# Meta tokens' products in four column quarters, attention inputs in two substeps, group sums by parity

## What is computed

```python
def first_block(...):                      # cut
    ...                                    # four mixers, x = x + rms_norm(y)
    h = rms_norm(x, pre_mlp_g[l])
    m = jnp.square(jax.nn.relu(h @ mlp_w1[l])) @ mlp_w2[l]
    x = x + rms_norm(m, post_mlp_g[l])

def second_block(...):                     # cut
    h = jnp.concatenate([meta, x], axis=1)            # 16 meta rows, then 256
    for layer in range(2):
        hn = rmsnorm(h, norm_mix[layer])
        if layer == 0:
            mix = pool_mixer(hn, pool_w[0], pool_scale[0])       # four column groups of 256
        else:
            q = rmsnorm((hn @ w_q[0]) by heads, q_norm[0])
            mix = stick_breaking(q, k_sh, v_sh) @ w_o[0]
        h = h + mix
        h = h + peer(rmsnorm(h, norm_ffn[layer]), peer_wq[layer], peer_keys[layer], ...)
        if layer == 0:
            kv = rmsnorm(h, kv_norm) @ w_kv           # keys and values for layer 1
    return h[:, N_META:]
```

## Time and profile before

| | |
|---|---|
| median of 3 timed runs | 1873.5 us (1872.88 to 1874.62) |
| profiled execution | 1869.93 us |
| its span, first to last instruction | 1867.8 us |
| mean granted TensorE clock | 0.829 of 2.4 GHz |
| busy: PE, DVE, ACT, POOL | 1380.9, 1166.1, 597.2, 548.5 us |
| HBM traffic | 678.30 MB read, 364 GB/s over the span |

### The profile page before, as it was taken

One profiled execution on the slowest core, in us unless ns is written; L12 is line 12 of the kernel. 1 busy time (PEld: TensorE's weight loads), 2 busy tenths in 40 slices (PEclk: granted clock), 3 DMA queues, 4 the chain that ended last, 5 costly groups with the idle time before them and its releaser, 6 DMA issues.

```text
span 1867.8 us, 21493 instructions
## 1 busy us (share of the span) xinstructions
PE 1380.9 (74%) x7036; PEld 559.3 (30%) x7036; DVE 1166.1 (62%) x2679; ACT 597.2 (32%) x1524; POOL 548.5 (29%) x629
## 2 busy tenths in 40 slices
PE   7979999987885556669777875596687855555666
PEld 6836666654330110123122221131232210101010
DVE  4831244037785767776688537866886478677764
ACT  2421011113443333344343333333543333332332
POOL 2001052003333333322333322332333233333332
PEclk9989999989996775689777897798897977766666
DMA  9049297617999999999999999999999999999997
GB/s 332 23 150 359 91 378 292 252 46 306 420 420 418 421 421 421 421 408 417 419 392 398 418 416 421 413 392 417 421 417 419 419 421 403 421 421 421 418 420 294
DMA packets 117982, 680.74 MB, mean 364 GB/s; under 512 B 11710, under 2 KB 13888, under 8 KB 49904
## 3 DMA queue, kind: packets, MB, share of 16 engines
q0 software_dynamic: 78336, 553.68, 71.9%
q1 hardware_dynamic: 39536, 125.71, 17.5%
HBM read 678.30 MB, written 1.05 MB: 364 GB/s over the span
## 4 chain that ended last, share of the span: by engine, by line
DMA 36%; PE 32%; DVE 12%; ACT 5%; issue 3%; DVEq 2%; POOL 2%; ACTq 1%; POOLq 0%
DMA big<-in_peer_uv,expert 32%; PE ps L585 7%; PE ps L743 6%; PE ps L1777 6%; PE ps L1788 6%; DVE big L598 6%; DMA normed<-in_peer_uv,expert 2%; DVEq L464 2%; DMA big<-in_w_kv 2%; PE ps L570 2%; POOL big L556 2%; PE ps L329 1%; ACT placed L633 1%; ACT placed L629 1%; ACT L606 1%
## 5 line engine op out<-in xcount | busy, mean ns | idle before, releaser
L585 PE MATMUL ps<-big,placed 128*32 128x512 f32 x1992 | 600.4, 802 | 383.1 <-ACT placed L633 381.4
L598 DVE CUSTOM_DVE_ANT_0 big<-big,ps 128x1024 f32<-128x1024 f32 x498 | 595.5, 1219 | 331.6 <-DMA big<-in_peer_uv,expert 316.7
L556 POOL DMA_INDIRECT big<-in_peer_uv,expert x498 | 472.3, 948 | 1033.0 <-PE ps L585 856.3
L629 ACT ACTIVATE placed<-sel,dots 128x32 f32<-128x32 f32 x512 | 163.4, 319 | 783.7 <-DVE dots L598 776.6
L585 PEld LDWEIGHTS ps<-big,placed 128*32 128x32 f32 x1992 | 82.2, 123 | 819.5 <-ACT placed L633 743.5
L743 PE MATMUL ps<-big 128*128 128x512 f32 x384 | 188.5, 627 | 13.6 <-DMA big<-in_w_kv 5.2
L633 ACT ACTIVATE placed<-placed,gate 128x32 f32<-128x32 f32 x512 | 164.6, 321 | 36.8 <-issue 2.1
L1777 PE MATMUL ps<-ua,big 128*128 128x256 f32 x512 | 117.5, 383 | 0.0
L1788 PE MATMUL ps<-big,sc 128*128 128x512 f32 x256 | 115.5, 595 | 0.0
L743 PEld LDWEIGHTS ps<-big 128*128 128x128 f32 x384 | 69.9, 196 | 129.2 <-issue 106.2
L1777 PEld LDWEIGHTS ps<-ua,big 128*128 128x128 f32 x512 | 98.5, 193 | 27.2 <-issue 15.0
(11 more groups left out here) (346 smaller groups left out, 1298.2 us busy)
## 6 DMA issues: line engine op xcount, KB each, us to landing
big<-in_mlp_w SPq DMA_DIRECT2D x16, 2048.0 KB, 12.0
big<-in_peer_wq SPq DMA_DIRECT2D x2, 8192.0 KB, 26.9
big<-in_w_kv SPq DMA_DIRECT2D x32, 512.0 KB, 15.7
big<-in_peer_wq SPq DMA_DIRECT2D x32, 512.0 KB, 14.6
big<-in_w_in SPq DMA_DIRECT2D x5, 2048.0 KB, 17.7
big<-in_peer_uv,expert POOLq DMA_INDIRECT x530, 14.9
big<-in_w_q SPq DMA_DIRECT2D x16, 512.0 KB, 11.7
big<-in_w_o SPq DMA_DIRECT2D x16, 512.0 KB, 11.9
```

Of the source, the lines that this page charges most:

```text
L556: nc.gpsimd.indirect_dma_start(out=pair_row(n), out_offset=None, in_=rows, in_offset=bass.IndirectOffsetOnAxis(ap=expert[:, n // TOPK % DE ...
L585: last = nc.tensor.matmul(acc[r:r + TOK, :], placed[:, n % RING, :], pair_row(n)[:, D + BANK * half:D + BANK * (half + 1)], start=(opens a ...
L598: nc.vector.tensor_tensor_reduce(out=row, in0=row, in1=rows_x, scale=1.0, scalar=0.0, op0=ALU.mult, op1=ALU.add, accum_out=dots[:, u % 2, ...
L629: a.activation(to, sel32[:], ACT.Gelu, scale=dots[:, u % 2, k:k + 1])
```

## The change

Meta part of the MLP: the pool products, the scores and the sum over heads are written as products that go to four partition quarters of one bank (rows 0, 32, 64, 96 on), each with at most 32 of the array's columns, ordered so that four neighbours use different columns. The zeroed operand of the scores (`q_meta`) shrinks from 2304 to 512 columns. DVE reads the results in four pieces. The product with `spread`, its table and ACT's copy are gone; instead SP copies the 16 meta rows eight times within the core's memory into `meta_x`, ahead of the load of w1's chunk 3 and behind a wait for the meta queries.

Attention: PE's row transposes go to banks 6 and 7 (meta rows to bank 4). DVE makes the query inputs (and the meta columns) at i = 1 and the key and value inputs at i = 2; PE's query products wait for the former alone, the key products for all. Stage 2 of unit 18's ranking moves from substep (16, 3) to (16, 2), where tile 1's norm stands too.

Group sums: `add_group` waits for the even slots' last product, adds their two quarters, then waits for the odd ones'.

```diff
+        q_meta = big[:, W + 2048:W + 2560].rearrange("p (w j c n) -> p w j c n", w=2, j=QUADS, c=2)
...
-                (16, 2): (18, (0, 1)), (16, 3): (18, (2, 3)), (22, 3): (24, (0, 1)), (23, 0): (24, (2, 3)),
+                (16, 2): (18, (0, 1, 2)), (16, 3): (18, (3,)), (22, 3): (24, (0, 1)), (23, 0): (24, (2, 3)),
...
-            slots_done(dve, "v_used", TOPK * (u + 1))
             for par in range(2):
+                slots_done(dve, "v_used", TOPK * (u + 1) - 1 + par)
...
             if i == AT_Q and q == 0:
-                pe.wait_ge(S("a_inputs"), ONE["a_inputs"] * t + 5 - t)
+                pe.wait_ge(S("a_inputs"), ONE["a_inputs"] * t + 3 - t)
...
+            if i == AT_K and q == 0:
+                pe.wait_ge(S("a_inputs"), ONE["a_inputs"] * t + 5 - t)
...
+        def attend_input(dve, to, gains, j):
+
+            gain = vec[:, gains + 4 * j:gains + 4 * j + 4].unsqueeze(2).broadcast_to([P, 4, P])
+            step(dve, nc.vector.tensor_tensor(to[:, 4 * j:4 * j + 4, :], cut(bank(6 + j), 0, 4, P), gain, ALU.mult), "a_inputs")
...
                 for j in range(2):
-                    for to, gains in uses:
...
+                    attend_input(dve, q_in, G_MIX1, j)
...
+            if i == 2:
+                for j in range(2):
+                    attend_input(dve, kv_in[t][:, :, META * (1 - t):], G_KV, j)
...
+                    if c == 3:
+                        sp.wait_ge(S("meta_q_done"), 1)
+                        for head in range(PH):
+                            sp.dma_start(meta_x[META * head:META * (head + 1), :], meta_rows).then_inc(S("meta_x_loaded"), 16)
...
-                    if q == 12:
-                        act.wait_ge(S("meta_x_done"), 1)
-                        a.activation(meta_x, meta_banks, ACT.Copy).then_inc(S("meta_x"), 1)
...
-                step(dve, v.tensor_tensor(meta_rows, meta_banks[0:META], meta_scale, ALU.mult), "dve_order")
+                for g in range(POOL_GROUPS):
+                    cols = slice(GW * g, GW * (g + 1))
+                    step(dve, v.tensor_tensor(meta_rows[:, cols], meta_bank[TOK * g:TOK * g + META, 0:GW], meta_scale[:, cols],
+                                              ALU.mult), "dve_order")
...
-                        for k in range(KD):
-                            last = m.matmul(meta_banks[0:META, GW * (k // 2):GW * (k // 2 + 1)], meta_pooled[:, k, :], meta_poolw[:, k, :],
-                                            start=(k % 2 == 0), stop=(k % 2 == 1))
+                        for k in range(2):
+                            for g in range(POOL_GROUPS):
+                                last = m.matmul(meta_bank[TOK * g:TOK * g + META, 0:GW], meta_pooled[:, 2 * g + k, :],
+                                                meta_poolw[:, 2 * g + k, :], start=(k == 0), stop=(k == 1))
...
-                            for head in range(PH):
-                                last = m.matmul(bank(7)[:, P * p:P * (p + 1)], q_meta[:, p, P * head:P * (head + 1)],
-                                                meta_keys[:, 2 * head + p, :], start=(head == 0), stop=(head == PH - 1))
+                            for c in range(2):
+                                for j in range(QUADS):
+                                    last = m.matmul(bank(7)[TOK * j:TOK * (j + 1), P * p:P * (p + 1)], q_meta[:, p, j, c, :],
+                                                    meta_keys[:, 2 * (2 * j + c) + p, :], start=(c == 0), stop=(c == 1))
...
-                    if q == 10:
-                        pe.wait_ge(S("spread_ready"), 1)
-                        pe.wait_ge(S("meta_scores_out"), 1)
-                        for c in range(2):
-                            last = m.matmul(bank(6 + c), spread, meta_rows[:, BANK * c:BANK * (c + 1)], start=True, stop=True)
-                        last.then_inc(S("meta_x_done"), 1)
...
-                        for c in range(2):
-                            last = m.matmul(bank(6 + c)[0:META], sel16[:], meta_sum[:, BANK * c:BANK * (c + 1)],
+                        for g in range(QUADS):
+                            last = m.matmul(meta_bank[TOK * g:TOK * g + META, 0:GW], sel16[:], meta_sum[:, GW * g:GW * (g + 1)],
                                             start=True, stop=True)
```

More of the change, by code:

```diff
@@ L167, in program @@
         KV0 = META + P
+        QUADS = 4
+        TOK = P // QUADS
         keys_t0 = gb[:, :, :].rearrange("p a (j n) -> p (a j) n", n=KEYS)
@@ L180, in program @@
         meta_t, meta_pooled = (cut(ua, 3776 + P * i, KD, META) for i in range(2))
-        spread = ua[0:META, 4032:4032 + P]
         meta_poolw = hn[:, :, :].rearrange("p t (a n) -> p (t a) n", n=GW)
@@ L763, in attend_pe @@
                 for k in range(KD):
-                    last = m.transpose(bank(4 + k // 4)[:, P * (k % 4):P * (k % 4 + 1)],
+                    last = m.transpose(bank(6 + k // 4)[:, P * (k % 4):P * (k % 4 + 1)],
                                        rows_n[:, P * k:P * (k + 1)], ident[:])
@@ L769, in attend_pe @@
                     for k in range(KD):
-                        last = m.transpose(bank(6)[:, META * k:META * (k + 1)], rows_m[:, P * k:P * (k + 1)],
+                        last = m.transpose(bank(4)[:, META * k:META * (k + 1)], rows_m[:, P * k:P * (k + 1)],
                                            ident[0:META, 0:META])
@@ L1063, in attend_dve @@
                 for j in range(2):
-                    for to, gains in uses:
-                        gain = vec[:, gains + 4 * j:gains + 4 * j + 4].unsqueeze(2).broadcast_to([P, 4, P])
-                        step(dve, v.tensor_tensor(to[:, 4 * j:4 * j + 4, :], cut(bank(4 + j), 0, 4, P), gain, ALU.mult),
-                             "a_inputs")
+                    attend_input(dve, q_in, G_MIX1, j)
                 if t == 0:
@@ L1070, in attend_dve @@
                     gain = vec[:, G_KV:G_KV + KD].unsqueeze(2).broadcast_to([P, KD, META])
-                    step(dve, v.tensor_tensor(kv_in[0][:, :, 0:META], cut(bank(6), 0, KD, META), gain, ALU.mult),
+                    step(dve, v.tensor_tensor(kv_in[0][:, :, 0:META], cut(bank(4), 0, KD, META), gain, ALU.mult),
                          "a_inputs")
+            if i == 2:
+                for j in range(2):
+                    attend_input(dve, kv_in[t][:, :, META * (1 - t):], G_KV, j)
             for n, at in enumerate((AT_Q + 1, AT_K + 1)):
@@ L1654, in _ @@
                 step(dve, v.memset(meta_q, 0.0), "dve_order")
-                step(dve, v.tensor_copy(spread.rearrange("p (h t) -> p h t", t=META),
-                                        ident[0:META, 0:META].unsqueeze(1).broadcast_to([META, PH, META])), "spread_ready")
                 dve.wait_ge(S("bands_ready"), 3 * POOL_GROUPS)
@@ L1708, in _ @@
                     for w in range(2):
-                        own = q_meta[:, w, :].rearrange("p (j c n) -> p j c n", c=2, n=HEAD)[:, :, c, 0:META]
+                        own = q_meta[:, w, :, c, META * c:META * (c + 1)]
                         part = bank(6)[:, P * (2 * c + w):P * (2 * c + w + 1)].rearrange("p (j n) -> p j n", n=TOK)
@@ L1715, in _ @@
                     route(dve, META_UNIT, stage)
-                dve.wait_ge(S("meta_x"), 1)
+                dve.wait_ge(S("meta_x_loaded"), 16 * PH)
                 for n in range(TOPK):
@@ L1737, in _ @@
                 dve.wait_ge(S("meta_summed"), 1)
-                step(dve, v.tensor_tensor(meta_h, meta_h, meta_banks[0:META], ALU.add), "meta_out")
+                for g in range(QUADS):
+                    own = meta_h[:, GW * g:GW * (g + 1)]
+                    step(dve, v.tensor_tensor(own, own, meta_bank[TOK * g:TOK * g + META, 0:GW], ALU.add), "meta_out")
                 dve.wait_ge(S("gain1_loaded"), 16)
@@ L1831, in meta_pe @@
                         for p in range(2):
-                            for head in range(PH):
-                                last = m.matmul(bank(7)[:, P * p:P * (p + 1)], q_meta[:, p, P * head:P * (head + 1)],
-                                                meta_keys[:, 2 * head + p, :], start=(head == 0), stop=(head == PH - 1))
+                            for c in range(2):
+                                for j in range(QUADS):
+                                    last = m.matmul(bank(7)[TOK * j:TOK * (j + 1), P * p:P * (p + 1)], q_meta[:, p, j, c, :],
+                                                    meta_keys[:, 2 * (2 * j + c) + p, :], start=(c == 0), stop=(c == 1))
                         last.then_inc(S("meta_scores_done"), 1)
-                    if q == 10:
-                        pe.wait_ge(S("spread_ready"), 1)
-                        pe.wait_ge(S("meta_scores_out"), 1)
-                        for c in range(2):
-                            last = m.matmul(bank(6 + c), spread, meta_rows[:, BANK * c:BANK * (c + 1)], start=True, stop=True)
-                        last.then_inc(S("meta_x_done"), 1)
                     if q == 25:
```

(5 more changed lines are left out.)

9 lines of the change are left out of this document (2 added, 7 removed).

## The result

The changed kernel takes 1861.36 us (median of 4 runs, 1859.01 to 1862.03) against 1873.88 us for the kernel before, timed beside it (4 runs, 1872.88 to 1874.62): a ratio of 0.993, 95% interval 0.9918 to 0.9943. The forecast was 1862.0 with a range of 1857.5 to 1866.5. The profiled execution took 1860.9 (span 1858.8, mean granted clock 0.832); forecast for it was 1858.4.

The account below looks back on a forecast made before the run. PE alone was taken to bound the MLP, memory transfers the stretch from the eleventh slice on. Gains 8.5 + 1.4 + 0.2 + 1.4 = 11.5 us took the median from 1873.5 to 1862.0, range 1857.5 to 1866.5.

Parts of the forecast that it names:

- MLP, 8.5: Meta blocks of the MLP: quarters save 2.67, 2.57 and 1.37 us, the dropped spreading 1.91; sum 8.5 us.
- the sign of being wrong: Start of the expert loop: the prediction is wrong if the first gather does not come 8.5 us sooner.
- Rival C: MLP meta blocks: quarters that use 16 columns run one after another; total gain 4.9 us, 1868.6; chance 0.06.
- Copies on SP: SP's queue: eight copies take 3.3 us to issue, w1's chunk 3 is issued at 204.4, no cost.
- rival D: SP's queue: the eight copies run in series and hold up w1's chunk 3 by 23 us; 1885; chance 0.04.
- Tile 1, 1.4: Attention at tile 1: query products start 1.43 us sooner and the 3.8 us transfer hole becomes 2.4; gain 1.4.
- the forecast's own lower bound: Tile 1, least gain: the moved ranking stage delays three gathers, opening a new hole of some 2.4 us; gain 1.4.
- rival B: Tile 1: the attention edit gives nothing, a new hole takes the old one's place; 1863.6; chance 0.19.
- PE warm: Tile 1, most gain: query products at full clock, no new hole, so all of the 3.8 us goes.
- Tile 0, 0.2: Attention at tile 0: the same shift of the query products, hole of 0.2 us; gain 0.2, from 0 to 1.
- Parity, 1.4: End of the kernel: two of the last four adds fit before PE's last product; gain 1.4 us, bounds 0.7 and 1.5.

Follow-up runs that it names:

- e3: Kernel before with only the group sums parity by parity: median 1872.17 us, ratio 0.9993.
- e2: Kernel before with only the attention inputs in two substeps and the moved ranking stage: median 1873.32 us, ratio 0.9999.
- e10: Kernel before with waits that are met at once added to TensorE's program ahead of the MLP: median 1876.56 us, ratio 1.0002.
- e4: Changed kernel with stage 2 of unit 18's ranking back in substep (16, 3): median 1861.41 us, ratio 0.9931.
- e8: Changed kernel with pool products and scores reordered so that neighbours in PE's queue lie in the same column quarter: median 1861.27 us, ratio 0.9928.
- e9: Changed kernel with the five attention products spread (one, two, two) instead of (two, two, one) over a unit's first three quarters: median 1864.75 us, ratio 0.9943.
- e11: Changed kernel with waits that are met at once added to ScalarE's program at three MLP steps: median 1861.98 us, ratio 0.9932.
- e6: Kernel before, unchanged, in a third profiled execution: 1871.87 us, one run.
- e7: Changed kernel with w1's chunk 3 held back on SP's queue until 12 up steps are done instead of 8: median 1881.48 us, ratio 1.0037.
- e1: Kernel before with only the meta part of the MLP (quarters, no spread product, copies on SP): median 1862.68 us, ratio 0.9939.
- e5: Kernel before, unchanged, in a second profiled execution: 1873.76 us, one run.
- e12: Kernel before with the quarters part and the parity-by-parity group sums, without the attention edit: median 1863.28 us, ratio 0.9939.

## Why the prediction was right, point by point

**MLP, 8.5.** Measured 8.3 by the blocks and 8.2 at the first gather, over the means. In the two profiles themselves the first gather came 9.38 us sooner (427.80 and 418.42), but the six kernels without quarters alone spread over 2.6 us there, so the sign of being wrong that I had set at 8.5, of which 8.2 falls just short, was finer than one pair of profiles can tell. The nearest rows, of 128 records of L329 and 16 of L364, priced the quarters well: 0.99 against 0.89, 1.01 against 1.0, 0.56 against 0.45. One sentence was wrong: that the trace shows no charge for changing to quarters and back. It does, 0.20 us, in the row of the block behind L1819, which I had not set beside its like. The sum didn't suffer, because only the scores had not paid it and the spreading took its own away. Rival C is excluded by the blocks.

**Copies on SP.** The issues took 0.63 us each instead of 0.41, and the chunk was issued at 205.98 instead of 204.4. No wait came of it. A transfer of 64 KB landed in 2.4 us (median of eight), not in the 5.6 from which rival D's series was made.

**Tile 1, 1.4.** The gap from the forecast's own lower bound came true in kind: a hole ahead of the query products, at 1192 to 1200, in place of the one behind them. It is 3.35 us and not 2.4 (by the same measure, H, the old one was 4.22 and not 3.8), and the step that failed is which gather is the first to be late. POOL in order of time, changed kernel and kernel before:

```profile
1185.83 0.94 POOL L554 DMA_INDIRECT big<-in_peer_uv,expert  x1 [0.30 <-PE ps L583]
...
1192.62 0.94 POOL L554 DMA_INDIRECT big<-in_peer_uv,expert  x1 [5.85 <-PE ps L583]
...
1196.36 0.94 POOL L554 DMA_INDIRECT big<-in_peer_uv,expert  x1 [2.80 <-PE ps L583]
```

```profile
1194.14 0.94 POOL L556 DMA_INDIRECT big<-in_peer_uv,expert  x1 [0.30 <-issue]
...
1196.62 0.94 POOL L556 DMA_INDIRECT big<-in_peer_uv,expert  x1 [1.54 <-PE ps L585]
```

The gather of 1196.62 waits for the product of the first of the four dots behind tile 1's norm, and the moved stage now stands ahead of that norm. With it the gather came 6.79 us behind the one before instead of 2.48. I had let the delay begin with the three from 1200.88 on, and those are late by the same 4 us. So the part gave 0.6 to 1.2 by the holes, and by its place the hole is the sign that I had set for rival B, though B had it as long as the old one. What I gave as the case against, PE warm and a hole ahead, both happened; I had taken them for alternatives.

**Tile 0, 0.2.** Too small for any of these runs.

**Parity, 1.4.** The end of the changed kernel, against the earlier trace rows, and that of e3:

```profile
1853.43 1.38 DVE L643 TENSOR_TENSOR residual<-residual,ps 32x512 f32<-32x512 f32 x2 [0.23 <-PE ps L583]
...
1854.01 1.05 PE L583 MATMUL ps<-big,placed 128*32 128x512 f32 x4 [0.62 <-ACT placed L631]
...
1855.11 1.39 DVE L643 TENSOR_TENSOR residual<-residual,ps 32x512 f32<-32x512 f32 x2 [0.29 <-PE ps L583]
1856.53 0.31 SPq L1568 DMA_DIRECT2D out<-residual  x1
```

```profile
1866.41 1.38 DVE L645 TENSOR_TENSOR residual<-residual,ps 32x512 f32<-32x512 f32 x2
...
1867.09 1.92 PE L585 MATMUL ps<-big,placed 128*32 128x512 f32 x4 [0.72 <-ACT placed L633]
...
1869.06 1.39 DVE L645 TENSOR_TENSOR residual<-residual,ps 32x512 f32<-32x512 f32 x2 [1.26 <-PE ps L585]
```

Two of the four adds stand before PE's last product ends, and E went from 7.08 to 5.63: 1.45. Forecast 1.4. The rest of the spread in column E is the clock of that last product. It takes 1.05 us at a granted clock of 1.00 (before, e2, e10; changed, e4, e8, e9, e11) and 1.92 at about 0.50 (e6; e3, e7), with e1, e5 and e12 between. At full clock E is 7.1 without parity and 5.6 with it, at half clock 7.96 (e6) and 6.50 (e3, e7): 1.46 both times. That is also why e3, alone, took 7.7 us from the last dot's start to the end, where 6.8 was expected; the changed kernel took 6.9. DVE reading one half of a bank beside PE's writing of the other cost nothing to be seen: 1.38 for two adds, as 2.85 for four.

**The sum against the median.** 11.5 forecast, 12.5 measured. The parts as they were found make 8.3, some 0.9, and 1.45: 10.7. Of the 1.8 that no part accounts for, 1.1 lies ahead of the 80th dot, where B averages 222.3 in the six profiles of the old code and 221.2 in the seven with quarters and no late chunk. The other 0.7 is inside the spread of the runs. I had kept the 3.6 us between the profiled execution and the median as a constant. It was not: the first profile of before was an execution without the delay in A, and the profiled one of the changed kernel had it. That is most of why the forecast for the profiled execution, 1858.4, was 2.5 too low, and the median came out 0.6 under the forecast. Two errors of a microsecond, the attention edit and this delay, have opposite signs, and the forecast looks better than its terms: that the median lies 0.6 us from it is in part luck. The range was also about 1 us wider on each side than the terms named for it make.

## What to carry to other kernels

Where a matmul fills few of the array's columns, quarters side by side are worth their full arithmetic: 3.56 us became 0.99. The price of going back to the whole array, 0.20 us, is in the row behind the block, so compare that row with its like. Before comparing two ends, or any two stretches, see that PE's granted clock was the same in both: here one product at half clock hid 0.9 of an edit's 1.4 us. Before building on one profiled execution, see whether it lies off the median; if it does, a second one shows which stretch makes the difference, and that stretch is no term of the change.

## What the runs showed that I had not expected

A transfer of 2 MB landed 8.7 us after its issue at 205.98, before the gathers of the meta rows, and 20.4 us after it at 230.29, beside them: a chunk held up into such a stretch is later than its delay. PE's first block after 15.8 us of idling took 5.29 us instead of 3.45.

Two matmuls in a row in the same quarter cost no more than two in different ones (1.05 against 1.01 us for 16).

In the first microseconds after the gathers have filled the queues an engine can lose 2 to 6 us with nothing in the trace that it waits for, in 13 of the 14 profiled executions, and at a place that padding a program did not move.
